# Attention: the last unit's output is transposed back behind the first block of probabilities of a unit, in place of the second

## What is computed

```python
logits = jnp.einsum('bqgrd,bqkgd->bqgrk', q.astype(F32), k_g) * ATT_HEAD_DIM ** -0.5
...
logits = logits - slopes[None, None, :, :, None] * dist[:, :, None, None, :]
logits = jnp.where(valid[:, :, None, None, :], logits, -jnp.inf)
p = jax.nn.softmax(logits, axis=-1)
out = jnp.einsum('bqgrk,bqkgd->bqgrd', p, v_g)
...
att = y_att.reshape(B, L, D_ATT) * jax.nn.silu(z_att)
```

## Time and profile before

| | us |
|---|---|
| median of 3 runs | 2708.27 (2708.1 to 2708.75) |
| the profiled execution's own time | 2710.26 |
| its span, first to last instruction | 2708.4 |
| TensorE busy (matmuls) | 2516.3 (93%) |
| VectorE busy | 1912.1 (71%) |
| ScalarE busy | 1410.7 (52%) |
| GpSimd busy | 772.2 (29%) |
| mean granted clock of TensorE | 0.975 of 2.4 GHz |

### The profile page before, as it was taken

One profiled execution on the slowest core, in us unless ns is written; L12 is line 12 of the kernel. 1 busy time (PEld: TensorE's weight loads), 2 busy tenths in 40 slices (PEclk: granted clock), 3 DMA queues, 4 the chain that ended last, 5 costly groups with the idle time before them and its releaser, 6 DMA issues. The chain is left out here.

```text
span 2708.4 us, 39667 instructions
## 1 busy us (share of the span) xinstructions
PE 2516.3 (93%) x14786; PEld 2188.1 (81%) x14787; DVE 1912.1 (71%) x3236; ACT 1410.7 (52%) x2559; POOL 772.2 (29%) x779
## 2 busy tenths in 40 slices
PE   7998979999999999998999957989999988899997
PEld 5887779999999888998966745777787777788886
DVE  3799878988998899548568855777676667444443
ACT  3678657677776651224455744655555555322221
POOL 0011324334344243345446753222121131000000
PEclk9999989999999999999999978999999999999999
DMA  7330063232235333367444442221110057322210
GB/s 244 115 99 4 1 213 101 87 96 93 79 92 174 120 101 94 107 210 234 150 156 156 164 161 83 72 59 49 43 43 24 26 160 249 124 94 94 94 63 24
DMA packets 187480, 294.70 MB, mean 109 GB/s; under 512 B 29450, under 2 KB 131733, under 8 KB 185750
## 3 DMA queue, kind: packets, MB, share of 16 engines
q1 hardware_dynamic: 164489, 220.30, 26.0%
q0 software_dynamic: 22800, 71.88, 7.4%
HBM read 181.92 MB, written 110.20 MB: 108 GB/s over the span
## 5 line engine op out<-in xcount | busy, mean ns | idle before, releaser
L797 PE MATMUL PS<-project_wh,project_xh 128*128 128x256 f32 x1224 | 347.1, 284 | 0.0
L797 PE MATMUL PS<-project_wh,project_xl 128*128 128x256 f32 x1224 | 346.4, 283 | 0.0
L797 PE MATMUL PS<-project_wl,project_xh 128*128 128x256 f32 x1224 | 346.4, 283 | 0.0
L797 PE MATMUL PS<-project_xh,project_wh 128*128 128x384 f32 (+1 forms) x880 | 315.2, 358 | 20.6 <-DMA project_xl<-x_parts 20.6
L797 PE MATMUL PS<-project_xl,project_wh 128*128 128x384 f32 (+1 forms) x880 | 314.9, 358 | 0.0
L797 PE MATMUL PS<-project_xh,project_wl 128*128 128x384 f32 (+1 forms) x880 | 314.8, 358 | 0.0
L2311 DVE TENSOR_TENSOR attend_ptl<-PS,attend_pth 128x512 fp32r<-128x512 f32 x272 | 185.2, 687 | 172.3 <-ACT attend_pth L2173 171.5
L909 DVE TENSOR_SCALAR_CACHE_REDUCE spare_spare<-all_S,project_cand 128x768 bf16<-128x768 f32 (+8 forms) x288 | 291.5, 1036 | 0.0
L2173 ACT CAST attend_pth<-PS 128x512 fp32r<-128x512 f32 x272 | 156.5, 582 | 165.1 <-PE PS L1991 159.3
L797 PEld LDWEIGHTS PS<-project_wl,project_xh 128*128 128x128 f32 x1224 | 234.4, 192 | 0.0
L797 PEld LDWEIGHTS PS<-project_wh,project_xh 128*128 128x128 f32 x1224 | 234.4, 192 | 0.0
(11 more groups left out here) (337 smaller groups left out, 6098.2 us busy)
## 6 DMA issues: line engine op xcount, KB each, us to landing
project_raw<-in_w_in SPq DMA_DIRECT2D x80, 512.0 KB, 3.9
featT<-project_st POOLq DMA_DIRECT2D x66, 192.0 KB, 2.4
all_S<-featT SPq DMA_DIRECT2D x12, 1024.0 KB, 6.1
featT<-project_st POOLq DMA_DIRECT2D x44, 256.0 KB, 2.3
x_parts<-index_s_x POOLq DMA_DIRECT2D x10, 1024.0 KB, 7.1
gate_s<-project_st POOLq DMA_DIRECT2D x68, 128.0 KB, 2.3
gate_a<-project_st POOLq DMA_DIRECT2D x68, 128.0 KB, 2.8
ssd_x<-x_tok SPq DMA_DIRECT2D x17, 512.0 KB, 5.0
```

Source lines behind the costliest of these rows:

```text
L797: last = nc.tensor.matmul(PS[:, r % 8, 0:w], lhsT, rhs, start=(k == 0 and j == 0), stop=(k == KT - 1 and j == 2))
```

## The change

`back(n - 1)` is called in the first iteration of a unit, not the second. For units 0 and 1, which have one block, nothing changes; in units 2 to 31 it moves.

```diff
                     for hc in range(turned, todo[done][0] if done < len(todo) else GH * (n + 2) if todo else turned):
                         exps(hc)
                         turned = hc + 1
-                    if n and kb == min(1, blocks - 1):
+                    if n and kb == 0:
                         back(n - 1)
                     upto = min(len(todo), -(-len(todo) * (kb + 1) // max(blocks - 2, 1)))
```

## The result

The kernel got slower: 2724.66 us (median of 4 runs, 2723.25 to 2726.1) against 2708.51 (4 runs beside them, 2708.1 to 2709.97), a ratio of 1.0053 with a 95% interval of 1.0041 to 1.0065. That is a loss of 14.4 us by the ratio (11.1 to 17.6), 16.2 by the two medians and 14.5 by the profiled executions. The prediction had the sign, but said 7.3 us, 2715.6, and at most 2721.

What follows compares the result with a forecast made beforehand. The prediction saw mostly TensorE's idle time in the attention stage to gain or lose. Its terms, 5.4 - 2.4 + 2.4 + 0.7 + 2.7 - 1.5, gave +7.3 us, a median of 2715.6, range 2706 to 2721.

Steps and rivals of the forecast that it cites:

- TensorE's new wait: At a unit's start the transposes back wait for the copy and start at 0.85: 0.49 us of new idle time.
- VectorE's new order: Normalisation, 1.30 us, stands between first low part and first mask-add, which starts at 3.21 instead of 2.03.
- Units 16 to 22, 24, 25: Units like 20, whose first product comes later: 0.6 us lost each, +5.4 in all, bounds 1.7 to 8.1.
- Units 2 to 5: Units 2 and 3 lose their normalisation wait, -2.4 us; units 4 and 5 get a later last product, +2.4.
- units 14, 28, 29 and 31: No third piece ahead of the first product; they gain the normalisation wait less the copy's 0.49: -1.5 us.
- the row of units 6, 8 to 13, 26, 27 and 30: Ends come through VectorE and ScalarE, whose work sum stays; casts queue later in some: +0.7 us, 0 to 1.5.
- The step that failed: GpSimd's gating, the store and SP's loads come earlier in unchanged queue order; costed at nothing.
- The term: Units 7, 15, 23: normalisation stands ahead of new keys' low parts; net 0.9 us each, +2.7, bounds 0 to 3.9.
- the rule on banks of the Trainium skill: Independent groups in different banks should overlap evacuation with matmuls; by it alone, new idle time of 30 x 0.49 = +14.7.
- Same: Rival: waits at the ends of units absorb the 5.4 loss, leaving +1.9 us, 2710.2; chance 0.25.
- faster: Rival: the 17.4 us normalisation wait goes and nothing follows; copy costs 10.8, so -6.6, 2701.7; chance 0.07.
- The clock falls at unit starts: Rival: new idle time lowers TensorE's clock in ten large units, 1 us each: +17, 2725; chance 0.06.

Runs made afterwards that it cites:

- the runs with units 7, 15, 23 mended: Two variants of the changed kernel: in these units GpSimd's gate waits for VectorE's splits, 2718.4 us; or these units keep the old place, 2715.82 us.
- The run in which GpSimd alone waits: Against the changed kernel, GpSimd's gate in units 7, 15 and 23 waits until VectorE's four splits are done; 2718.4 us.
- the run with VectorE's old order: Against the changed kernel, TensorE's transposes stay early but VectorE's normalisation goes back behind its work on block 1; 2729.86 us.
- the run with query parts beside the splits: Against the kernel before, GpSimd in units 7, 15 and 23 makes later query parts beside VectorE's splits, not behind its gate; 2712.91 us.
- the run with both behind the first pieces: Against the changed kernel, TensorE's transposes and VectorE's normalisation go behind a unit's first score pieces, ahead of the second block; 2707.28 us.
- the one with units 2 and 3 early: Transposes and normalisation behind the first score pieces, but in units 2 and 3 directly behind block 0 as in the changed kernel; 2706.07 us.

## Why the prediction was right and wrong

*Right, by its own steps.* TensorE's new wait: 24 waits of the transposes for the copy, 0.24 each; the transposes start at 0.83 to 0.88 from the start of units 5 to 31 (0.85). VectorE's new order: the mask-add of unit 20 starts at 3.21, the first product at 5.99 (5.98). Units 16 to 22, 24, 25: 5.3 (5.4). Units 2 to 5: unit 3 only 0.7 shorter and unit 2 1.6, together 2.3 (2.4); units 4 and 5 +1.4 and +1.7 (1.2 each), in the runs with units 7, 15, 23 mended +1.0 and +1.2. Units 10 to 13 +0.0 to +0.2, unit 26 +0.4 (as long as before for all of them). The waits for mask-adds 10.8 (over 8), for the normalisation 1.1 (under 3).

*Luck in it.* The -2.3 of units 2 and 3 fits by luck in part: in the four other runs in which these units have the order of the change they were 3.1, 1.8, 1.6 and 1.4 shorter. Of the -2.5 of units 14, 28, 29 and 31, unit 31 has 2.1, of which 1.5 is the clock of that execution (last section). And the row of units 6, 8 to 13, 26, 27 and 30 came to +2.3, over its bound of 1.5, with units 26 and 27 at a granted clock of 0.98 and 0.95 (1.00 before).

*The step that failed* is this passage: "Gating on GpSimd, the store and the loads behind it on SP keep their places in their queues and come earlier; I cost that at nothing". The signals were costed, the resources were not: in units 7, 15 and 23 "earlier" means beside VectorE's splits. The price is 2.55 us of VectorE's time a unit on the path to the first piece, and behind the longer stall a longer stretch at the lower clock (unit 15: 0.93 before, 0.82 after). The term was +2.7 with a bound of 3.9; it measured +10.1, and with GpSimd kept out of the way +2.0 (-0.1, +1.9 and +0.1, where 0.9 each was forecast). The run in which GpSimd alone waits lost about 7.3 us (5.1 to 9.8), as the forecast had it without this cost; the sum agrees better than its rows, for the reasons just given.

The trace of the kernel before had the sign in it, at a place that the change doesn't touch. The first four splits of the stage have GpSimd beside them:

```profile
1603.48 1.51 DVE L2277 TENSOR_TENSOR attend_kl<-attend_lg,attend_kh 128x512 fp32r<-128x512 f32 x2
1603.71 1.81 POOL L1886 TENSOR_TENSOR attend_bias<-attend_ndist,attend_mask 128x128 f32<-128x128 f32 x2 [3.41 <-DVE attend_ndist L2270]
...
1604.91 2.17 DVE L2282 TENSOR_TENSOR attend_vl<-attend_lg,attend_vh 128x512 fp32r<-128x512 f32 x2
1605.46 1.07 POOL L1875 CAST attend_qh<-attend_qraw 128x512 fp32r<-128x512 f32 x1
1606.62 1.59 POOL L1877 TENSOR_TENSOR attend_ql<-attend_qraw,attend_qh 128x512 fp32r<-128x512 f32 x1
```

They take 3.60 us (1603.48 to 1604.91 + 2.17), where those of unit 15 take 2.48, and GpSimd's cast takes 1.07 in place of 0.62.

The Trainium skill states the mechanism (SBUF — State Buffer, Who interferes with whom): VectorE and GpSimd share a pair of SBUF ports under an exclusive lock, and a VectorE instruction with two inputs in SBUF contends with a GpSimd instruction that reads SBUF; whichever comes first holds it, the other "fully blocks". The traces agree: 1.75 in place of 0.68 for a split that came behind the gate, 0.61 unchanged for a cast that came first. It also says that an instruction with at most one SBUF input doesn't contend (outside some modes); here the mask-add of unit 20, with scores in PSUM, takes 1.22 beside the gate, as the 1.23 in the earlier trace rows. The prediction left this rule out, though it speaks against the change in three units.

*The attribution in units 16 to 25* was half right. The size and the path came out (mask-add, third piece, product). But the prediction put the mask-add's delay down to VectorE's order alone (1.31 + 0.60 + 1.30), though by its own sum the first piece starts only at 1.20 and ends at 2.68. TensorE's wait and transposes ahead of the first piece would make the mask-add 0.88 late by themselves, and the normalisation adds 0.30: it fills most of a hole that TensorE has made.

By the rule on banks of the Trainium skill (Perfetto Trace Analysis, Optimizing Tensor Performance, Matmuls) the prediction had estimated +14.7. That it lies next to the measured 14.4 is luck. Ten of the 16.0 us in the lengths of units come from three units and another cause, and the others range from -2.1 to +1.7. Where nothing fills the hole, in the run with VectorE's old order (18 us), most units lose the wait and the transposes' time together, 0.65 to 0.92 each.

*The rivals.* "Same" and "faster" are out by the time. The waits at the ends of units didn't absorb the loss: they rose from 17.6 to 21.4 in all, and in units 16 to 22, 24 and 25 they are 5.6 in both traces. "The clock falls at unit starts" named 2725, close to what came, but not for its reason: the clock explains TensorE's 5.8 us of extra busy time, scattered over units 4 to 6, 15 and 26 to 28, and the 0.49 of idle time at the start of units 16 to 22, 24 and 25 lowered it in none of them (1.00 throughout). The 26 "longer waits" of the argument against it are too many: 18 of them are longer than 0.49.

## What to carry to other kernels

Work that comes earlier on an engine off the path isn't free: list what then runs beside it on VectorE and GpSimd, above all VectorE instructions with both inputs in SBUF. One kind of instruction with two durations in one trace, as the splits at 1603.48 and in unit 15 before the change, is the sign to look for. And when an instruction moves ahead of a piece of TensorE's work, follow the first consumer of that piece before the moved instruction's own chain: here 0.9 us of delay came from there, and the place behind the first piece, which hides the same wait, lost nothing.

## What was unexpected of the hardware

The blocking is mutual: in unit 15 VectorE's splits grew by 2.55 us, and GpSimd's gate, cast, subtraction and bias together by 1.5 (7.27 busy, 5.76 before).

The clock after one and the same wait can differ from one execution to the next. Unit 31 before the change, and in the run with query parts beside the splits, where this unit has the same order:

```profile
2193.86 0.57 PE L2001 MATMUL PS<-attend_pth,attend_vh 128*128 128x512 f32 x1 [2.11 <-DVE attend_att L2321]
2194.23 0.63 PE L2001 MATMUL PS<-attend_pth,attend_vl 128*128 128x512 f32 x1
```

```profile
2196.66 0.47 PE L2004 MATMUL PS<-attend_pth,attend_vh 128*128 128x512 f32 x1 [2.12 <-DVE attend_att L2324]
2196.97 0.40 PE L2004 MATMUL PS<-attend_pth,attend_vl 128*128 128x512 f32 x1
```

After 2.11 us of idle time the same matmul takes 0.63 in the one and 0.40 in the other. The granted clock of the 2 us behind the wait is 0.55 in the one, so mostly 1.2 GHz, and 1.00, 2.4 GHz, in the other; unit 31 is 1.6 us shorter there. After the change's wait of 1.08 it took 0.40 in each of the six profiles that have it. So of the 2.1 us that unit 31 gained only 0.6 is the earlier product (4.04 and 3.45 from the start); the rest was the clock of that execution. Units 26 and 27 show the like: +0.6 and +2.2 in the run with both behind the first pieces (granted clock 0.98 and 0.93), 0.0 in the one with units 2 and 3 early (1.00), with the same order there.
